# Two of 59 paired weight transfers asked for in pieces of 112, 8 and 8 rows

## The reference, cut to what matters

```python
h = x + mix
h = h + moe(rmsnorm(h, norm_ffn), ...)      # top-4 of 32 experts

def expert_block(args):                     # for each expert e
    xb, e = args
    h = xb @ w_up[e] + b_up[e]              # w_up[e]:   1024 x 2048 float32, 8 MB
    h_glu = jnp.minimum(h[:, :D_FF], SWIGLU_LIMIT)
    h_lin = jnp.clip(h[:, D_FF:], -SWIGLU_LIMIT, SWIGLU_LIMIT)
    act = h_glu * jax.nn.sigmoid(SWIGLU_ALPHA * h_glu) * (h_lin + 1.0)
    return act @ w_down[e] + b_down[e]      # w_down[e]: 1024 x 1024 float32, 4 MB
```

## Time and profile before

| what | value |
| --- | --- |
| median of 3 runs | 1098.51 us (1098.44 to 1102.69) |
| the profiled execution's own time | 1097.69 us |
| span of the profile | 1095.8 us |
| TensorE busy | 1067.1 us, 97% |
| VectorE busy | 359.0 us, 33% |
| ScalarE busy | 152.7 us, 14% |
| moved by DMA | 431.47 MB, mean 394 GB/s |
| granted TensorE clock | 0.998 |

### The profile page before, as it was taken

One profiled execution on the slowest core, in us unless ns is written; L12 is line 12 of the kernel. 1 busy time (PEld: TensorE's weight loads), 2 busy tenths in 40 slices (PEclk: granted clock), 3 DMA queues, 4 the chain that ended last, 5 costly groups with the idle time before them and its releaser, 6 DMA issues.

```text
span 1095.8 us, 13185 instructions
## 1 busy us (share of the span) xinstructions
PE 1067.1 (97%) x5681; PEld 449.5 (41%) x5682; DVE 359.0 (33%) x567; ACT 152.7 (14%) x302; POOL 12.1 (1%) x28
## 2 busy tenths in 40 slices
PE   8999999999999999999999999999999999999997
PEld 6888754333333333333333333333333333333332
DVE  3454634322222222222222222223322222232234
ACT  2021144111111111111111101111111011011113
POOL 1000000000000000000000000000000000000002
PEclk9999999999999999999999999999999999999999
DMA  8675948999999999999999999999999999999994
GB/s 291 230 271 193 388 159 343 412 429 426 432 429 427 436 429 430 431 432 429 429 431 430 430 430 433 424 435 430 426 435 432 427 432 429 425 429 426 427 415 157
DMA packets 43931, 431.47 MB, mean 394 GB/s; under 512 B 4792, under 2 KB 20188, under 8 KB 25440
## 3 DMA queue, kind: packets, MB, share of 16 engines
q1 hardware_dynamic: 43264, 430.41, 93.8%
q10 hardware_dynamic: 608, 0.20, 0.1%
HBM read 427.00 MB, written 3.48 MB: 393 GB/s over the span
## 4 chain that ended last, share of the span: by engine, by line
PE 79%; DMA 19%; issue 0%; DVE 0%; ACT 0%; POOLq 0%; DVEq 0%; POOL 0%; ACTq 0%
PE bank L977 34%; DMA ring_all<-in_w_up 15%; PE bank L996 15%; PE bank L672 9%; PE bank L1041 5%; PE bank L951 4%; DMA ring_all<-in_w_down 3%; PE bank L988 2%; PE bank L781 2%; PE bank L959 2%; PE bank L969 1%; PE bank L634 1%; PE bank L1034 1%; PE bank L1053 1%; PE bank L789 1%; PE bank L1079 1%
## 5 line engine op out<-in xcount | busy, mean ns | idle before, releaser
L977 PE MATMUL bank<-ring_all,work 128*64 128x512 f32 x2048 | 484.9, 600 | 13.0 <-DMA ring_all<-in_w_up 12.9
L977 PEld LDWEIGHTS bank<-ring_all,work 128*64 128x64 f32 x2048 | 135.4, 136 | 263.0 <-issue 252.6
L996 PE MATMUL bank<-ring_all,work 128*64 128x512 f32 x992 | 225.4, 596 | 0.8 <-DMA ring_all<-in_w_down 0.8
L1786 DVE TENSOR_TENSOR h_tok<-h_tok,bank 128x1024 f32<-128x1024 f32 (+1 forms) x67 | 81.8, 1220 | 243.0 <-PE bank L1041 237.2
L996 PEld LDWEIGHTS bank<-ring_all,work 128*64 128x64 f32 x992 | 68.5, 137 | 129.7 <-issue 128.8
L672 PE MATMUL bank<-work,ring_all 128*128 128x264 f32 x384 | 87.0, 387 | 1.0 <-DVE h_tok L1577 1.0
L1756 DVE TENSOR_TENSOR work<-bank,bias_up 128x1024 f32<-128x1024 f32 x32 | 39.2, 1224 | 124.7 <-PE bank L988 124.7
L672 PEld LDWEIGHTS bank<-work,ring_all 128*128 128x128 f32 x384 | 72.5, 190 | 13.3 <-DVE h_tok L1577 1.2
L1041 PE MATMUL bank<-work 64*128 64x512 f32 (+1 forms) x268 | 75.1, 637 | 0.0
L1773 DVE TENSOR_TENSOR work<-work 128x512 f32<-128x512 f32 x32 | 22.2, 692 | 108.3 <-ACT work L1378 108.2
L1362 ACT ACTIVATE work<-bank 128x264 f32<-128x264 f32 x32 | 12.5, 391 | 316.3 <-PE bank L969 316.3
(11 more groups left out here) (226 smaller groups left out, 547.1 us busy)
## 6 DMA issues: line engine op xcount, KB each, us to landing
ring_all<-in_w_up SPq DMA_DIRECT2D x44, 4096.0 KB, 33.4
ring_all<-in_w_up SPq DMA_DIRECT2D x33, 2048.0 KB, 18.4
ring_all<-in_w_down SPq DMA_DIRECT2D x15, 4096.0 KB, 33.1
ring_all<-in_w_down SPq DMA_DIRECT2D x28, 2048.0 KB, 33.3
ring_all<-in_w_up SPq DMA_DIRECT2D x14, 1024.0 KB, 10.2
ring_all<-in_w_in SPq DMA_DIRECT2D x13, 1024.0 KB, 5.0
ring_all<-in_w_down SPq DMA_DIRECT2D x12, 1024.0 KB, 9.9
ring_all<-in_w_out SPq DMA_DIRECT2D x4, 1024.0 KB, 10.6
```

Of the source, the lines that this page charges most:

```text
L977: mm = pe.matmul(bank[half * CAP:(half + 1) * CAP, up_bank(n) + b, :].rearrange("q (k p) -> q p k", k=KT), x, src[:, half * FF + b * 512:h ...
L996: mm = pe.matmul(bank[half * CAP:(half + 1) * CAP, Y, :], av[:, 2 * i + k, :], src[:, k * D + half * 512:k * D + (half + 1) * 512], start= ...
L1786: tt(rows, rows, bank[0:m, b:b + 2, :], ALU.add).then_inc(comb_added, 1)
```

## The change

Two of the 59 paired transfers are asked for in several instructions instead of one, each for some of the rows: the pair at the first chunk of `w_up` of expert 10 in rows 0 to 111, 112 to 119 and 120 to 127, and that of expert 19 in rows 0 to 111, 112 to 119, 120 to 126 and 127. All pieces of a pair add 16 each to the same semaphore, so that the count TensorE waits for grows by 48 or 64 there. The bytes, their places, the order of the chunks and the waits of SP are the same. Both places are such that the pair begins exactly at chunk u,n,0 (chunks 58 and 112 of the stream).

```diff
 PAIRED = (6, 28)
+SHIFT = {10: ((0, 112), (112, 120), (120, 128)), 19: ((0, 112), (112, 120), (120, 127), (127, 128))}
...
         pairs = [s for s in range(place["u", PAIRED[0], 0], place["u", PAIRED[1], 0], 2) if s % RING < RING - 1]
+        shifted = {next(s for s in pairs if s >= place["u", n, 0]): parts for n, parts in SHIFT.items()}
         signal, seen = [], [0] * RING
...
-            seen[s % RING] += 1
+            seen[s % RING] += len(shifted.get(s, (0,)))
             signal.append((s % RING, 16 * seen[s % RING]))
...
                     if s in pairs:
                         sp.wait_ge(mm_done, s - RING + 2)
-                        sp.dma_start(ring_all[:, s % RING:s % RING + 2, :].rearrange("p a n -> p (a n)"),
-                                     pair_src(stream[s])).then_inc(landed[s % RING], 16)
+                        for p0, p1 in shifted.get(s, ((0, P),)):
+                            sp.dma_start(ring_all[p0:p1, s % RING:s % RING + 2, :].rearrange("p a n -> p (a n)"),
+                                         pair_src(stream[s])[p0:p1]).then_inc(landed[s % RING], 16)
                         continue
```

## The result

The changed kernel takes 1137.78 us (median of four runs, 1135.38 to 1143.14), the one before 1098.47 us in the same comparison (1098.33 to 1102.69). The ratio is 1.0358, with a 95% interval of 1.0338 to 1.0379: 39.3 us slower. The forecast was 1110.5 us, and the range ended at 1117 us.

The account below looks back on a forecast made before the run. Weight transfers, paced by the latest DMA engine, were taken to bound the kernel from about 570 us. 0 + 0 + 11.0 + 1 = +12 us on 1097.69, plus 0.8 to the median, gave 1110.5 us; range 1095.5 to 1117 us.

Parts of the forecast that it names:

- What bounds the kernel: Whole stream: TensorE lives on the ring's stock until about 570 us, then transfers set the pace; at most 13.7 us recoverable.
- Steps 1 and 2: At both split pairs: extra instructions on SP and higher semaphore counts cost 0; without cover, instructions 1 us at most.
- Step 3: At both pairs: lower eight engines get nine rows, upper eight seven, at 1.22 us a row; upper 2.4 us earlier.
- The lead: About eight engines finish the weights some 5.8 us before the others; some 1.5 us at the first changed place.
- Step 4: At both pairs: eight-row pieces run slower, lower engines lose 16.8 us, ending 11.0 us later than the former latest.
- the 112-row piece: Large piece of each split pair: uneven shares can cost another row, 1.22 us a pair; 1 us added with shorter lead.
- The eights: Eight-row pieces of the split pairs: 4.8 us each at the 8-row store's 55 GB/s, against 1.22 us at full pace.
- the loss of the upper engines: Upper engines sharing rows with a piece lose 3.8 us and save 1.22; +5 us over two pairs, not deciding.
- TensorE's part: TensorE's waits on weight transfers rise from 13.7 us to about 25 us and begin before 570 us.
- The balance rival: At both pairs: pieces run at full pace, late upper engines gain, end 2.4 us earlier at 1096.1 us; chance 0.28.
- The shape that I named for my own forecast: Behind chunks 58 and 112: some 10 us of GB/s well below 430 at share near 1, waits before 570 us.

Follow-up runs that it names:

- e1: The changed kernel with only expert 10's pair split (112, 8, 8 rows), expert 19's pair one request again: 1122.35 us.
- e8: The changed kernel with both pairs cut into 64 even rows, 32 and 16 odd rows and two spread eight-row pieces: 1106.31 us.
- e12: The changed kernel with only expert 10's pair cut, into 16 pieces of eight rows lying four apart: 1119.92 us.
- e14: The changed kernel with both pairs cut into 64 even rows, 32 odd rows and four eight-row pieces, rows four apart: 1114.66 us.
- e2: The changed kernel with both pairs cut into 112 and 16 neighbouring rows, no row moved between engines: 1131.78 us.
- e11: The changed kernel with only expert 10's pair cut, into 16 pieces of eight neighbouring rows: 1138.64 us.
- e6: The changed kernel with both pairs cut into eight pieces of 16 rows, every eighth row each: 1137.88 us.
- e7: The changed kernel with both pairs cut into 96 and 32 neighbouring rows: 1127.55 us.
- e15: The changed kernel with both pairs cut into 48 even and 48 odd rows below 96, and the last 32 rows: 1125.34 us.
- e3: The changed kernel with both pairs cut into two halves of 64 neighbouring rows: 1129.75 us.
- e9: The changed kernel with both pairs cut into 64 even rows, 32 odd, 16 over all row groups and two spread eights: 1107.4 us (median).
- e13: The changed kernel with both pairs cut into 64 even rows, 32 odd rows and two 16-row pieces by fours, no row moved: 1106.29 us.

## Why the prediction was wrong, point by point

**What bounds the kernel.** Right. The dents in the stream come out at the end nearly in full: 34.6 us of missing bytes, 40.3 us of span. TensorE ran dry within the first dent (busy 0 from 440 to 450 us), so the stock in the ring didn't cover even the first one.

**Steps 1 and 2, instructions and semaphores, cost 0.** Right: four pieces that reach all groups cost 0.1 us.

**Step 3, rows moved, -2.4 us for the upper engines.** The price of a moved row, 1.22 us, was right; the gain from it came in no run. Seven kernels gave the lower engines more rows (e1, e8 to e12, e14), and all were slower. The lead that I put at some 1.5 us at the first place is there on average, 0.8 to 1.2 us, but not on every lower engine, and the latest of them decides. Whether the eight that are done early at the end are the lower ones, no run shows.

**Step 4, the pace of a piece with few rows.** This failed, and at one term: "What I can't bound closely is the 112-row piece [...] which can cost another row or so (1.22 us) a pair", for which, with a shorter lead, I added 1 us. I looked for the price in the two pieces of eight and took the large one to run at full pace. The windows show it at half, 216 to 249 GB/s. At half pace an engine's seven rows take 7 x 1.22 = 8.5 us more, 17 us over two places; the upper end of my range, 1119 us, allowed some 4 us for it. That term is the one that took the time out of the range. The packets of e2 agree: 16.6 us for the seven rows instead of 8.5. By the experiments the 112-row piece and one of 16 are 30.7 of the 39.7 us, and cutting the 16 into eights, or 8, 7 and 1, is 9.0.

I had the rule in hand. I had read in the earlier trace rows that 64 rows run at half pace, and had written that the shares of seven "no longer fall on the same groups of rows". I then bounded the effect by one row instead of by that row of the trace: half pace for the whole piece. The nearest row for a large piece of fewer than 128 rows was that of 209 GB/s, and it should have been the upper bound.

The other two terms. The eights, taken at 4.8 us each, were about right: on the one lower engine of the changed kernel that can be joined whole at the first place they took 3.7 and 4.2 us. They took less where nothing but eights was in the pair: 3.1 us on average in e11, and 2.5 us or 1.2 us with spread rows. What I had too low is the loss of the upper engines in the meantime. I gave it to the engines that share rows with a piece; but all weight rows that start from 434 to 441 us took 3.7 to 4.5 us, whichever engine had them. And the lead of 5.8 us, which I subtracted, gave nothing back that a run shows. It was an error by itself: the eight engines that are done early were not shown to be the ones that get more rows.

One term was missing altogether, the pair behind. Its eight rows took 12.1 to 12.5 us instead of 9.7 in e2, e6, e7 and e15, and 11.8 us in e3, that is 2 to 3 us a place. On that lower engine of the changed kernel the seven rows took 15.2 us, the eights 3.7 and 4.2 us, and the pair behind 12.3 us, 35.4 us for what took 19.5 before. That is 16 of the 20 us or so of a place. The last rows of the pair before, 1.3 to 2.2 us each on several engines, are a part of the rest. Why the pieces of 112, 96 and 48 rows lose a whole half, and why rows of every engine take 4 us while eights of neighbouring rows are under way, stays open.

**TensorE's part.** I forecast waits of about 25 us; they were 46.4 us, and 8.0 us more of busy time that I hadn't forecast. After 10 us without a matmul the granted clock is 0.50 in the window from 445 us and 0.60 in the next, so the first matmuls run at 1.2 GHz instead of 2.4. It doesn't look like a cost of its own here: e11 ends as late as the changed kernel (1136.7 against 1136.1 us) with only 4.2 us more of busy time (1071.3) and 49.2 us of waits. What the clock takes, the waits seem to give back as long as the transfers are behind; no run varied the clock alone.

**The rivals.** The balance rival had 0.28. Its first condition, pieces at full pace, held only for spread eights in rows 0 to 63, and its second, a lead on each lower engine, didn't hold. The shape that I named for my own forecast came out: stretches of low GB/s at a share near 1, behind both chunks, and waits before 570 us. They lasted 35 to 40 us instead of 10.

## What to carry to other kernels

Cut a transfer of 128 rows in a full stream into every second or every fourth row, if it has to be cut: that was free. 64, 96 or 112 neighbouring rows ran at half pace and cost some 15 us for 4 MB, and so did 48 rows taken by twos; pieces of 16 or 8 rows were free only in some rows. When one piece of a cut is small and looks suspicious, price the large one too, with the same row of the trace. Before you subtract a lead, make sure that the engine which gets the work is the one that has it. And before comparing single executions, look when the changed place begins: here a delay of 3.4 to 3.8 us from elsewhere lay ahead of it in four of them.

## What the runs showed of the hardware

- Pieces of 112, 96, 64 or 48 rows that are uneven over the groups move 203 to 249 GB/s at a share near 1: half of the 431 GB/s of a full transfer. For 112, 96 and 48 rows it wasn't told apart whether the spread or the number of rows does it.
- Splitting as such is free: four DMA instructions for one 4 MB pair, 1097.59 us against 1097.31 us before.
- Eight-row pieces with rows four apart took 1.2 us each in rows 0 to 63 and 2.5 us each in rows 64 to 127 (e12). A 16-row piece took 1.4 to 1.6 us spread over all 16 groups (e9) and 2.1 to 2.2 us on eight (e13).
- While slow pieces are under way all engines are slow: 203 to 213 GB/s at a share of 1 with rows four apart in rows 64 to 127, 131 GB/s at 0.9 with neighbours. The full transfer behind such a pair is slowed too, 12.1 to 12.5 us instead of 9.7.
